# A hybrid pooling / recurrent / SwiGLU layer on eight cores: new order tables, transfers planned at 265 GB/s, gate weights in four pieces, tile loads that wait for weight loads

## What is computed

```
h = RMSNorm(x);  u_pool | u_rnn | u_gate | g_pool | g_rnn = h @ W_in
y_pool = pool_mixer(u_pool) @ W_pool_out          windows 2, 4, 8, 16; per group a 128x128 map
v      = causal conv4(u_rnn)
r, i   = sigmoid(v @ block_diag(w_a) + b_a), sigmoid(v @ block_diag(w_x) + b_x)
a      = exp(-8 r softplus(-lam));  hr_t = a_t hr_{t-1} + sqrt(1 - a_t^2) i_t v_t
x      = x + (sigmoid(g_pool) y_pool + sigmoid(g_rnn) ((hr * gelu(u_gate)) @ W_rnn_out)) @ W_o
x      = x + (silu(h2 @ Wg) * (h2 @ Wu)) @ W_ffn_out,  h2 = RMSNorm(x)
out    = RMSNorm(x)
```

## Time and profile before

| | |
|---|---|
| median of the runs | 1025.53 us |
| lowest run | 1024.29 us |
| the profiled execution | 1024.35 us |
| its span on the slowest core (core 3) | 1022.8 us |
| outside the span | 1.55 us |
| spans of role a (cores 0, 2, 4, 6) | 1017.9, 1016.8, 1017.4, 1021.7 us |
| spans of role b (cores 1, 3, 5, 7) | 1022.7, 1022.8, 1022.7, 1022.4 us |
| role b, core 3: PE, DVE, ACT, POOL busy | 924.4, 591.4, 556.7, 336.8 us |
| role a, core 0: PE, DVE, ACT, POOL busy | 980.3, 526.9, 446.9, 214.6 us |
| SP's queue / POOL's queue, core 3 | 32.48 MB / 63.45 MB written |

### The profile page before, as it was taken

How to read it: one execution, slowest core, us unless ns; L and a number is a source line. 1 busy time by engine, 2 the same in 40 slices (tenths; PEclk the granted TensorE clock), 3 DMA queues, 4 the chain that set the end, 5 groups by cost and what they waited for, 6 DMA issues and landing times.

```text
span 1022.8 us, 13708 instructions; the slowest of 8 cores (1016.8 to 1022.8 us)
## 1 busy us (share of the span) xinstructions
PE 924.4 (90%) x4484; PEld 446.6 (44%) x4484; DVE 591.4 (58%) x798; ACT 556.7 (54%) x804; POOL 336.8 (33%) x347
## 2 busy tenths in 40 slices
PE   2378688698978999999999999999999999999995
PEld 1134233233433444444444444444555555555553
DVE  2179998999999867844253544533644452222235
ACT  2579997989889942548264938611722351111112
POOL 2438593778655641151001122112251211000000
PEclk8579789899989999999999999999999999999998
DMA  8921452003644276768403257255939175910003
GB/s 176 242 69 33 160 93 42 12 1 55 116 82 87 38 192 118 160 98 150 82 8 56 39 80 141 44 101 123 253 69 212 30 129 108 211 41 2 1 1 135
DMA packets 42765, 96.88 MB, mean 95 GB/s; under 512 B 3776, under 2 KB 19264, under 8 KB 42560
## 3 DMA queue, kind: packets, MB, share of 16 engines
q0 software_dynamic: 23904, 63.45, 36.1%
q1 hardware_dynamic: 18784, 32.48, 10.6%
HBM read 151.75 MB, written 7.60 MB: 156 GB/s over the span
## 4 chain that ended last, share of the span: by engine, by line
PE 78%; ACT 9%; issue 5%; POOL 3%; DVE 2%; DMA 2%; ACTq 0%; DVEq 0%; SPq 0%; POOLq 0%
PE bank L705 74%; PE bank L770 2%; PE bank L667 2%; DMA wu<-w_in 2%; ACT th L780 1%; DVE v L757 1%; ACT q L798 1%; POOL sq L638 1%; ACT th L788 1%; ACT v L745 1%; ACT L798 1%; ACT L780 1%; DMA xt<-xT 1%; POOL vb L765 1%; ACT wi L780 0%
## 5 line engine op out<-in xcount | busy, mean ns | idle before, releaser
L705 PE MATMUL bank<-h,wf 128*128 128x508 bf16 (+2 forms) x1408 | 280.7, 358 | 0.0
L705 PEld LDWEIGHTS bank<-h,wf 128*128 128x128 bf16 x1408 | 136.5, 97 | 139.9 <-issue 0.8
L757 DVE SCALAR_TENSOR_TENSOR v<-bank,keep_cst,v 128x496 f32<-128x496 f32 (+3 forms) x200 | 128.8, 683 | 32.4 <-POOL v L754 13.4
L705 PE MATMUL bank<-h,wu 128*128 128x500 bf16 (+4 forms) x576 | 130.1, 381 | 16.3 <-DMA wu<-w_in 11.0
L1084 DVE TENSOR_TENSOR ff<-tf,bank 128x508 bf16<-128x508 f32 (+2 forms) x88 | 55.7, 634 | 147.9 <-PE bank L705 123.5
L705 PE MATMUL bank<-ff,wz 128*128 128x508 bf16 (+2 forms) x704 | 139.5, 359 | 0.0
L1079 ACT ACTIVATE tf<-bank 128x508 f32<-128x508 f32 (+2 forms) x88 | 48.8, 557 | 137.8 <-PE bank L705 134.4
L652 ACT ACTIVATE sq<-x 128x508 f32<-128x508 f32 (+2 forms) x56 | 32.9, 590 | 125.3 <-DVE x L1096 97.4
L705 PEld LDWEIGHTS bank<-ff,wz 128*128 128x128 bf16 x704 | 68.9, 98 | 68.6 <-issue 0.5
L705 PEld LDWEIGHTS bank<-h,wu 128*128 128x128 bf16 x576 | 58.7, 103 | 83.9 <-issue 32.9
L765 POOL CAST vb<-v 128x496 bf16<-128x496 f32 (+3 forms) x68 | 61.1, 905 | 61.4 <-DVE v L757 53.3
(11 more groups left out here) (103 smaller groups left out, 1311.7 us busy)
## 6 DMA issues: line engine op xcount, KB each, us to landing
wf<-wfi POOLq DMA_DIRECT2D x44, 512.0 KB, 9.5
wz<-wfo POOLq DMA_DIRECT2D x16, 704.0 KB, 10.1
xt<-xT SPq DMA_DIRECT2D x16, 500.0 KB, 8.6
wu<-w_in POOLq DMA_DIRECT2D x16, 256.0 KB, 13.7
xt<-xT SPq DMA_DIRECT2D x8, 512.0 KB, 21.1
wa<-w_in POOLq DMA_DIRECT2D x16, 256.0 KB, 5.9
wg<-w_in POOLq DMA_DIRECT2D x16, 256.0 KB, 5.4
wb<-w_in POOLq DMA_DIRECT2D x16, 256.0 KB, 5.5
```

What stands on the lines that cost most here:

```text
L705: last = e.matmul(p.tensor[:, 0:n], lhsT=wap(kc), rhs=rhs(kc), start=(kc == 0), stop=(kc == K - 1))
L757: g.op("dve", c_dve(w), k, lambda e, p=p, o=o, w=w, s=s: e.scalar_tensor_tensor(out=v.tensor[:, o:o + w], in0=p.tensor[:, HALO - s:HALO - ...
```

## The change

1. New tables for both roles (all keys, windows, penalties). `dma_rate` goes from 185000 to 265000 bytes/us, `dma_lat` from 2.2 to 2.3; the lead of weight loads stays 34.89 in role a and goes from 16.65 to 11.44 in role b. The prefix of role b becomes [256, 508, 496, 496, 484]. All other tile widths stay.
2. `keep_rg` becomes four buffers of two heads each (`load_rg`), laid out so that each is contiguous per partition. The first is loaded in the head, the others behind the branch, each at a key of its own.
3. `signals` adds a wait to each tile load behind the head: for the last weight load that the plan has landed 4 us before the tile's transfer begins and that is issued before it.
4. `find_bank`, `banks` and `rnn_pair` are new: where a group has exactly two tiles of equal width, and no other special treatment, both tiles share a pair of neighbouring PSUM banks, and the convolution, the cast and the tanh work on both tiles in one instruction. The words "single tiles throughout" in the change's name belong to an entry `join=0` of the tables, which no code reads.
5. The planned cost of L757 rises by 0.045 us, that of the scan by 0.06 us.

```diff
+    def find_bank(self, b, t):
+        free = [self.bank_live[i] is None and self.banks[i][0] <= t for i in range(8)]
+        if b.space == "ps2":
+            c = [(max(self.banks[i][0], self.banks[i + 1][0]), i) for i in range(0, 8, 2) if free[i] and free[i + 1]]
+        else:
+            c = [(self.bank_live[i ^ 1] is None, self.banks[i][0], i) for i in range(8) if free[i]]
+        return min(c)[-1] if c else None
...
+        weights = sorted([o for o in self.order["pool"] if o.nbytes], key=lambda o: o.end)
+        for o in self.order["sp"][sum(h.eng == "sp" for h in self.head):]:
+            if o.nbytes and o.tag != "out":
+                begin = o.end - self.prm["dma_lat"] - o.nbytes / self.prm["dma_rate"]
+                t = [x for x in weights if x.end <= begin - 4.0 and x.start < o.start]
+                if t:
+                    o.deps.append(t[-1])
...
-        self.rg = rg = self.buf("keep_rg", [2, 8, 128], BF16)
+        self.rg = [self.buf("keep_rg", [2, 2, 128], BF16) for _ in range(4)]
...
             if j == 0:
-                head.append(self.load("pool", rg, lambda: rg.tensor[:], dr["rg"], 128 * 2048 * 4, K, "rg"))
+                head.append(self.load_rg(0, K))
...
+        both = len(tiles) == 2 and tiles[0][1] == tiles[1][1] and not (ps or on[2] or on[5])
+        if both:
+            self.rnn_pair(j, tiles, wu, key, toff, v, th, wi, kk_vb)
+        for i, (h, w, part) in enumerate([] if both else tiles):
...
+    def rnn_pair(self, j, tiles, wu, key, toff, v, th, wi, cast):
+        g, cst = self.g, self.cst
+        w = tiles[0][1]
+        two = lambda b: b.tensor[:].rearrange("p (t w) -> p t w", t=2)
+        p = self.banks("ps_u")
+        for i, (h, _, part) in enumerate(tiles):
+            self.mm_group(p, w + HALO, wu, lambda kc, h=h: h[kc // 2].tensor[:, kc % 2, 0:w + HALO],
+                          [(h[kc // 2], kc % 2) for kc in range(8)], key + toff * i, "u", wap=lambda kc: wu.tensor[:, kc, :], half=i)
+        k = key + toff
+        pk, vk = [(p, 0), (p, 1)], [(v, 0), (v, 1)]
+        g.op("act", c_act(2 * w, 2), k, lambda e: e.activation(
+            out=two(v), in_=p.tensor[:, :, HALO:HALO + w], func=AF.Identity,
+            scale=cst.tensor[:, C_CW + 24 + j:C_CW + 25 + j], bias=cst.tensor[:, C_CB + j:C_CB + j + 1]),
+            rd=pk + [cst], wr=vk, tag="v0")
+        for s in (1, 2, 3):
+            g.op("dve", c_dve(2 * w) + 0.05, k, lambda e, s=s: e.scalar_tensor_tensor(
+                out=two(v), in0=p.tensor[:, :, HALO - s:HALO - s + w],
...
-        begin=dict(pe=6.0, act=4.0, dve=3.0, pool=9.0, sp=9.5), window=72.67, table_pen=78.88, dma_rate=185000.0, dma_lat=2.2,
+        begin=dict(pe=6.0, act=4.0, dve=3.0, pool=9.0, sp=9.5), window=74.28, table_pen=83.59, dma_rate=265000.0, dma_lat=2.3,
...
-        prefix=[256, 496, 496, 496, 496], groups=[2, 2, 1], own=[[508, 508], [460, 380]], wp=261.84, window2=107.54,
+        prefix=[256, 508, 496, 496, 484], groups=[2, 2, 1], own=[[508, 508], [460, 380]], wp=275.48, window2=139.98,
```

132 lines of the change are left out of this document (78 added, 54 removed).

## The result

The changed kernel takes 1037.86 us (median; 1036.39 to 1040.9), the kernel before 1025.19 us on the same chips. The ratio is 1.0128, with an interval from 1.0111 to 1.0146: some 1.3% slower, where 0.8% faster was forecast, and outside the predicted range.

A forecast was written before the change was run, and what follows sets the result against it. VectorE was taken to bound role b from 75 to 350 us, TensorE role a from 125. Core 6, 1021.7 − 4 − 2 = 1015.7, ends last, role b at 1010.6; with 1.55 outside the span 1017.3 us, range 1007 to 1030.

The forecast's parts named there:

- The bound from 75 to 350: Role b from 75 to 350 us: VectorE, busy 260.8 of 275 us, stays the bound, so 10.2 us saved count in full.
- costing the new keys at nothing: The new keys reorder role a's tail, where TensorE has no gap: counted as 0, bounds −2 and 1.
- The pairs: Role b's prefix second group and first own chunk: 48 DVE instructions less at 0.21 us, 10.2 us won, bounds 0 and 14.
- The start, role a: Role a's first weights come earlier through a smaller `keep_rg` load and held-back tile pieces: 4 us won, bounds 0 and 5.
- The `wu` step: Start of core 0: of TensorE's wait for a `wu` until 24.11 up to 5.0 us can go, of that until 17.96 at most 0.8.
- The start, role b: Role b's start, where the second tile's norm decides: 2 us won, bounds −3 and 5.
- Core 6: Core 6 of role a, 3.8 us behind core 0, gains 2 us more with less in flight at POOL's branch, bounds 0 and 3.8.
- Behind some 342 us TensorE is never short of work: Role b's later part: TensorE is busy 648.67 of 650 us from 350 to 1000.
- A: Rival, chance 0.20: the start gives nothing, as the second tile is later by what the `wu` are earlier; 1022 to 1024 us.
- B: Rival, chance 0.13: the start gives more, core 6's lag goes and TensorE's clock doesn't fall from 25 to 50; 1004 to 1012.
- C: Rival, chance 0.12: in role b ScalarE's double starts wait for both tiles' projections, 3.8 us each time VectorE runs dry; 1031.
- D: Rival, chance 0.05: weights land late under the new planned rate and lead, up to 3.2 us per load; 1024 to 1028.

The follow-up runs named there:

- E2: The changed kernel without the new waits of tile loads, order the same: role a 1016.5, role b 1035.1 us, ratio 1.0122 to the kernel before.
- E13: The changed kernel with role a held back some 40 us by 18 tiny transfers before its first load: role b 1028.3 us; ratio 1.0253, set by role a.
- E14: The kernel before with role a held back by 18 tiny transfers before its first load: role b 1019.3 us, role a 1051.5; no ratio.
- E1: The changed kernel, order kept, each double instruction of a pair issued as two single halves: role b 1035.1 us, ratio 1.0163 to the kernel before.
- E3: The kernel before with only the new waits of tile loads added: role a 1025.8, role b 1020.1 us, ratio 1.0051.
- E12: The changed kernel with the new waits of tile loads in role b only: role a 1015.8, role b 1038.4 us, ratio 1.0173 to the kernel before.
- E8: The changed kernel, role b's fourth-tile squares and sums moved later, waits in role b only: role b 1040.4 us, ratio 1.0175 to before.
- E9: The changed kernel, role b's fourth-tile squares and sums moved later, no tile-load waits: role b 1036.7 us, ratio 1.0147 to before.

## Why the prediction was wrong

**The bound from 75 to 350.** The step that failed is "so it stays the bound and the 10.2 count in full", together with costing the new keys at nothing in role b (I gave them bounds of −2 and 1, for role a's tail alone). The forecast had role b's `wr` point some 12 us earlier, at 355.5; it came at 371.9. Of the 22.6 us between the 1010.6 of the sum and core 3's 1033.2, 16.4 are there and 6.2 behind it. VectorE was the bound at 94.8% busy only under an order that kept it fed. The new one takes role b's keys, lead and transfer rate all at once, and it feeds VectorE at 89.1%. That the order loses by itself is shown by E2 (not the waits), E13 and E14 (9 us between the orders with role a out of the way) and E1 (not the issuing of pairs). What in the making of the order is at fault (keys, rate, tile widths, or the pairs, pieces and costs as the planner sees them) is not shown. I had read the order only at the places where I looked for gains.

**The pairs.** Sign right, size wrong twice. The term was 10.2 us; E1 measures 5.5 busy, and at role b's end a microsecond or so that isn't clear of the scatter. The 0.21 came from mean durations at two widths, but instructions that stand back to back overlap in the records: the earlier trace rows have 33.0 us busy for 48, 0.69 each, against a mean of 734 ns, and so the fixed share was counted with the overlap in it. By means, two singles and one double differ by 2 x 735 − 1269 = 201 ns; by busy time by 2 x 677 − 1250 = 104. Busy time over count wouldn't have mended the estimate from two widths: it gives 0.69 at 508 and 0.46 at 256, so 0.23 us fixed, since the taps of 256 columns stand less close together. The Trainium skill ("VectorE: DVE Perf Modes", section "The TRN2 errata — SBUF-src ops pay a fixed extra latency per instruction") has some 120 cycles for it, by my estimate 0.125 us, and 6.0 in the sum; the 0.115 measured agree with it, and I weighed it against a row that didn't measure the same thing. The rest of the saving went elsewhere: VectorE's busy time to the `wr` point fell by 2.1 us only, as the scans of 1016 columns rose from 2402 ns in the mean to 2846 and those of 992 from 2400 to 2494 (below, before and then after; in E1, without pairs, they are at 2804 and 2636, so it comes with the order). ScalarE lost 3.9 us busy, not 14.

```profile
L828 DVE TENSOR_TENSOR_SCAN wi<-th,keep_hst,q 128x1016 f32<-128x1016 f32 x8 | 19.2, 2402 | 2.5 <-POOL q L822 2.3
```

```profile
L855 DVE TENSOR_TENSOR_SCAN wi<-th,keep_hst,q 128x1016 f32<-128x1016 f32 x8 | 22.6, 2846 | 3.3 <-POOL q L849 3.2
```

**The start, role a.** The `wu` step held: on core 0 TensorE waits 1.4 us for a `wu` in all, until 21.8, where it had waited 9.5, until 24.11. But "bounds 0 and 5" had no loss in it. What is late next, named in the prediction as the second tile, was underrated: E2 shows role a 6.3 us better without the waits, E3 7.3 worse with them. ScalarE's squares on core 0 now stand 12.1 us for tile pieces that are held back, where they stood 0.5 before and stand 1.2 in E2.

**The start, role b.** Right in sign and more than right in size up to 75 us on core 3: the norm of tile 2 at 46.5, the first scan 11.4 us earlier (on the four cores 10 to 12). Worth 2 in the sum; nothing of it reached the end, since part of it is work that was only put off, and VectorE then idles 9.9 us more between that scan and `wr`.

**Core 6.** The term of 2 us was wrong in kind, since it read one execution as a property of the core. Over the 56 other executions of before, core 6 ends at 1018.9 in the mean, like cores 2 and 4 (1018.9 and 1018.7), and is the last of role a in 11 of them; the last of the four, whichever it is, ends 1.8 us behind their mean. Nor does the time at which POOL leaves the branch tell the end: in after core 6 idles 3.90 us there and ends at 1023.3, core 0 idles 7.68 and ends at 1019.6.

**Behind the `wr` point.** "Behind some 342 us TensorE is never short of work" was taken over for an order that I hadn't looked at there. Core 3 takes 661.3 us for it in the place of 655.1, in E13 and E14 661.5 and 655.1. Of these 6.2 us, 1.3 are gaps that the waits name (beside 2.1 at the last sum in both: 1.3 in one before, 2.6 in six now), 1.3 a table load on ScalarE that now stands between the last sum and the last `ln`, 2.9 are counted as TensorE's busy time for the same 3317 matmuls. The rest is in the gaps too short to be listed. Why the same matmuls are busy 2.9 us longer isn't shown.

```profile
1022.16 1.16 PE L691 MATMUL bank<-acc,keep_ones 128*128 128x380 f32 x2 [2.08 <-DVE acc L679]
1023.39 1.28 ACT L695 ACT_TABLE_LOAD   x1 [2.04 <-PE bank L691]
```

**The rivals.** A's mechanism, that one transfer's gain is another's loss, is there, within role a (the `wu` against the second tile) and between the roles (E3, E12). That nothing would be won in sum was my own inference from the rule of turns; the totals agree with it, 241 GB/s before and 234 after from 25 to 50 us. B's clock gain hardly came where it was looked for (0.50 to 0.59 from 25 to 50 on core 3), but behind it (0.75 to 1.00 from 50 to 75), and didn't reach the end. C had the nearest number and its sign in the waits, and E1 refutes its mechanism: a view that shows the wait which a rival forecasts is no proof while something else can make the same wait. D is refuted as put: TensorE waits for no transfer behind the start. The missing rival was the plain one: the order itself is worse on the chip than in the plan. Of the prediction's own signs, two for "right" came (waits for `wu` on core 0 under 5 us, taps of 1016 columns at 1.27 us) and two for "wrong" (`wr` at 366 or later, the slowest core of role b).

**What stays open.** Why the new order idles more between 75 and 350 us of core 3 isn't settled (VectorE idles 5.5 us more than before from 75 to 200 and 10.4 more from 200 to 350). It isn't the issuing of pairs (E1), the waits (E2), the squares of tile 4 (E8, E9), nor mainly the transfers of role a (E13, E14); single keys, the new tile widths, and the pairs, pieces and raised costs as inputs of the planner weren't tried one by one. A plan that is searched anew with a truer cost of the start (POOL at the branch above all) wasn't tried either.

## What to carry to other kernels

When a list order is searched anew, the order is the change: print the plan beside the measurement for the old and the new kernel, the total and some points on the way, and distrust a gain that only the plan shows. Price joined instructions by the busy time of both forms, not by mean durations and not from two widths, and ask of a "bound" engine what keeps it fed. Don't build a term on a core that is late in one execution. Where two programs run side by side, read every run by role: what holds back one role's transfers can cost that role and help the other.

## What the runs showed of the hardware

- Cores that share no data still slow each other: role b's unchanged instructions end 4.6 us later when role a's waits go, with the second tile's norm on core 3 at 51.38 in the place of 46.52 (E12 against after), and 5.5 (after) or 3.3 us (before) earlier when role a starts 40 us later (E13, E14). Which cores share, and what, these runs don't tell.
- POOL's way out of the branch is idle time that no view puts down to anything. On role a's cores it lasts 3.28, 3.30, 5.24 and 10.35 us before and 3.90 to 7.68 in after; on role b's it is 9.7 to 9.8 on cores 1, 3 and 7 before, 12.28 and 14.18 on cores 7 and 3 in after, and up to 16.51 (core 7, E12). In E13, with role a's transfers held back behind the head, it is still 11.49 on core 5. What POOL waits for isn't shown.
- Joining two taps into one instruction of twice the columns saves 0.115 us on VectorE (E1).
- From 25 to 50 us core 3 wrote 234 GB/s at a DMA share of 1.02, near the 241 of before. Holding loads back changed what came first, not the total.
